# The S5 layer spread over the four retention heads, in quarters of four state tiles, with its tables built on VectorE a step ahead

## The reference, cut to what matters

```
q, k, v, g, u = split(xn @ w_in)                # 512 columns each
o_ret, s_new = retention(rope(q), rope(k), v)   # 4 heads, decay gamma_h, chunkwise
y_ret = silu(g) * head_layernorm(o_ret)
bu = einsum(u, B_bar)                           # S5: 32 groups of 16 channels, 64 complex states
h[t] = a_bar * h[t-1] + bu[t]                   # diagonal, complex
y = gelu(Re(C h) + D u); y_s5 = y * sigmoid(y @ w_glu + b)
x = x + concat(y_ret, y_s5) @ w_out
```

## Time and profile before

| | us |
|---|---|
| median of 3 runs (lowest, highest) | 2462.33 (2460.72, 2467.35) |
| profiled execution: its own time | 2461.94 |
| profiled execution: span | 2460.2 |
| PE busy | 2294.2 |
| DVE busy | 1215.8 |
| POOL busy | 1220.9 |
| ACT busy | 339.8 |

### The profile page before, as it was taken

How to read it: one execution, slowest core, us unless ns; L and a number is a source line. 1 busy time by engine, 2 the same in 40 slices (tenths; PEclk the granted TensorE clock), 3 DMA queues, 4 the chain that set the end, 5 groups by cost and what they waited for, 6 DMA issues and landing times.

```text
span 2460.2 us, 39360 instructions
## 1 busy us (share of the span) xinstructions
PE 2294.2 (93%) x16133; PEld 2123.2 (86%) x16133; DVE 1215.8 (49%) x2104; ACT 339.8 (14%) x578; POOL 1220.9 (50%) x1185
## 2 busy tenths in 40 slices
PE   7968768999999999999999989999989999999997
PEld 7967667997999999999999965687569799999996
DVE  6675576432535263674756425441543327253363
ACT  4211301212200000120110131110212210000001
POOL 5535676642665566666656500022025256655562
PEclk8988889999999999999999977889889999999998
DMA  5212323310222222233333321332131012222221
GB/s 189 85 69 86 103 99 121 138 69 35 70 86 86 86 76 78 85 118 141 130 144 148 113 104 52 131 131 86 56 137 69 35 69 73 83 86 86 84 71 54
DMA packets 36594, 231.27 MB, mean 94 GB/s; under 512 B 4332, under 2 KB 7404, under 8 KB 10864
## 3 DMA queue, kind: packets, MB, share of 16 engines
q1 hardware_dynamic: 21600, 154.15, 17.8%
q10 hardware_dynamic: 14864, 75.21, 7.8%
HBM read 195.50 MB, written 33.85 MB: 93 GB/s over the span
## 4 chain that ended last, share of the span: by engine, by line
PE 79%; DVE 16%; issue 2%; ACT 2%; DMA 0%; ACTq 0%; DVEq 0%
PE psum L513 60%; PE psum L543 14%; PE psum L529 2%; DVE hl L1899 1%; DVE xnl L1425 1%; DVE hh L1895 1%; DVE xc L1964 1%; PE psum L539 1%; DVE tm L1625 1%; DVE ss L1410 0%; DVE hr L1888 0%; DVE hs L1891 0%; DVE bbq L1649 0%; DVE tm L2178 0%; DVE tm L2177 0%
## 5 line engine op out<-in xcount | busy, mean ns | idle before, releaser
L463 POOL TENSOR_SCALAR whi<-raw 128x512 fp32r<-128x512 f32 x584 | 422.7, 724 | 1150.1 <-PE psum L513 1107.2
L465 POOL TENSOR_TENSOR wlo<-raw,whi 128x512 fp32r<-128x512 f32 x584 | 803.0, 1375 | 48.7
L513 PE MATMUL psum<-xnh,whi 128*128 128x288 f32 (+1 forms) x2816 | 625.5, 300 | 64.2 <-DVE xnl L1425 17.8
L513 PE MATMUL psum<-xnl,whi 128*128 128x288 f32 (+1 forms) x2816 | 618.7, 298 | 0.0
L513 PE MATMUL psum<-xnh,wlo 128*128 128x288 f32 (+1 forms) x2816 | 618.2, 298 | 0.0
L513 PEld LDWEIGHTS psum<-xnh,whi 128*128 128x128 f32 x2816 | 465.5, 192 | 74.2 <-issue 52.2
L513 PEld LDWEIGHTS psum<-xnl,whi 128*128 128x128 f32 x2816 | 464.9, 192 | 0.0
L513 PEld LDWEIGHTS psum<-xnh,wlo 128*128 128x128 f32 x2816 | 464.4, 191 | 0.0
L513 PE MATMUL psum<-hh,whi 128*128 128x288 f32 x1024 | 220.2, 296 | 1.6 <-DVE hl L1899 1.6
L513 PE MATMUL psum<-hl,whi 128*128 128x288 f32 x1024 | 219.3, 295 | 0.0
L513 PE MATMUL psum<-hh,wlo 128*128 128x288 f32 x1024 | 219.3, 295 | 0.0
(11 more groups left out here) (395 smaller groups left out, 2735.0 us busy)
## 6 DMA issues: line engine op xcount, KB each, us to landing
raw<-in_w SPq DMA_DIRECT2D x146, 1024.0 KB, 4.7
C<-in_C ACTq DMA_DIRECT2D x4, 1024.0 KB, 4.8
o_cp<-mvt ACTq DMA_DIRECT2D x4, 1024.0 KB, 3.9
o_cs<-C ACTq DMA_DIRECT2D x4, 1024.0 KB, 3.9
t_xc<-xc ACTq DMA_DIRECT2D x3, 1152.0 KB, 6.5
t_z<-mv ACTq DMA_DIRECT2D x3, 1152.0 KB, 4.1
t_q<-mq ACTq DMA_DIRECT2D x3, 1152.0 KB, 4.1
t_k<-mk ACTq DMA_DIRECT2D x3, 1152.0 KB, 4.2
```

Source lines behind the costliest of these rows:

```text
L463: pool.tensor_scalar(whi[:, s, c], raw[:, s, c], 1.0, 1.0, ALU.mult, ALU.mult).then_inc(S("slab_hi"), 1)
L465: ins = pool.tensor_tensor(wlo[:, s, c], raw[:, s, c], whi[:, s, c].bitcast(F32), ALU.subtract)
L513: ins = pe.matmul(bank(g, 2 * m + b)[:, 0:t1 - t0], W[wi][:, kk, m0 + m, :], r[:, kk, t0:t1], start=(at_first and wi == 0 and r is rh), st ...
```

## The change

Each quarter of S5, four of its sixteen state tiles, is put inside one retention head. A head is now, on PE: `score`, transposes of the quarter's input rows, `aux`, memory slab 4h, the quarter's kernel and states (`s5_states`), `out`, slab 4h+1, `mean`, slab 4h+2, `var`, the quarter's output (`s5_out`), slab 4h+3. In head 2 the states come ahead of the slab. DVE does `rotate_back` ahead of `out`'s evacuation, the scan behind it, `rotate_forward` behind the subtraction of the mean, and then the input rows, decay columns and output rows of the next quarter. The states stay in `za` and `zc` (two buffers each), so that `he` and `hf` go. Tables are a quarter in size, the memory tokens have tiles of their own (`memx`), and the decay table of the heads has two buffers that are reloaded. Of the seven doublings four stand behind the evacuation of v's first group, two behind that of its second, and the last behind that of g's first group.

```
@@ schedule() @@
     for h in range(RET_H):
         g("ret", h, "score")
-        if h:
-            g("ret", h - 1, "var")
+        g("s5", h, "T")
         g("ret", h, "aux")
-        for x, m in zip(("out", "mean"), MEM_RET[h]):
-            s("mem", *m)
-            g("mem", *m)
-            g("ret", h, x)
-    memory(8)
-    g("ret", RET_H - 1, "var")
-    memory(9)
-    g("s5T", 0)
-    g("s5T", 1)
-    g("s5K")
...
+        if h != 2:
+            memory(4 * h)
+        g("s5", h, "G")
+        if h == 2:
+            memory(4 * h)
+        g("ret", h, "out")
+        memory(4 * h + 1)
+        g("ret", h, "mean")
+        memory(4 * h + 2)
+        g("ret", h, "var")
+        g("s5", h, "Y")
+        memory(4 * h + 3)
@@ TensorE @@
+            def s5_states(j):
+                g = GR["s5", j, "G"]
+                pe.wait_ge(S("ca_ready"), j + 1)
                 group_open(pe, g)
...
+                pe.wait_ge(S("bt_ready"), j + 1)
...
+            for h in range(RET_H):
+                ret_score(h)
+                s5_transposed(h)
+                ret_aux(h)
+                if h != 2:
+                    memory(MEM_SLABS[4 * h])
+                s5_states(h)
+                if h == 2:
+                    memory(MEM_SLABS[4 * h])
+                ret_out(h)
+                memory(MEM_SLABS[4 * h + 1])
+                ret_mean(h)
+                memory(MEM_SLABS[4 * h + 2])
+                ret_var(h)
+                s5_out(h)
+                memory(MEM_SLABS[4 * h + 3])
@@ ScalarE @@
+            silu(0)
             group_ready(act, GR["rs", "g", 1])
-            act.wait_ge(S("memx_loaded"), 32)
             high_memory(0)
+            silu(1)
             for h in range(RET_H):
-                for m in MEM_RET[h]:
-                    memory_out(m)
+                input_rows_turned(h)
+                memory_out(MEM_SLABS[4 * h])
...
                 act.wait_ge(S("ret_c"), h + 1)
...
+                memory_out(MEM_SLABS[4 * h + 2])
+                rstd(GR["ret", h, "var"], rs)
+                gelu(h)
+                memory_out(MEM_SLABS[4 * h + 3])
+                if h == 1:
+                    act.wait_ge(S("memx1_loaded"), 32)
                     high_memory(1)
@@ VectorE @@
+                for n in ((1, 2, 4, 8), (16, 32))[i]:
+                    doubling(n)
+                    if n in (4, 32):
+                        unit_circle()
...
+            def scan_states(j):
+                A_, C_ = za[:, j % 2, :, 1:W5 + 1], zc[:, j % 2, :, 1:W5 + 1]
+                step(lambda: tt(A_, A_, zb[:], ADD), lambda: tt(C_, C_, zd[:], SUB))
...
+                step(*[lambda z=z: v.tensor_tensor_scan(flat(z[:, j % 2]), flat(rt[:]), flat(z[:, j % 2]), 0.0, MUL, ADD)
+                       for z in (za, zc)])
...
             for h in range(RET_H):
...
+                if h == 0:
+                    output_rows(0)
+                if h == 2:
+                    low_memory(1)
+                    rotate_back(h)
                     ret_y(h - 1)
-                memory_keys(MEM_RET[h][0])
+                    memory_keys(MEM_SLABS[4 * h])
+                else:
+                    if h:
+                        ret_y(h - 1)
+                    memory_keys(MEM_SLABS[4 * h])
+                    rotate_back(h)
...
+                scan_states(h)
+                memory_keys(MEM_SLABS[4 * h + 1])
...
+                rotate_forward(h)
+                memory_keys(MEM_SLABS[4 * h + 2])
+                if h + 1 < RET_H:
+                    input_rows(h + 1)
+                    decay_columns(h + 1)
+                    output_rows(h + 1)
+                else:
+                    split_glu(0)
+                    split_glu(1)
+                memory_keys(MEM_SLABS[4 * h + 3])
```

More of the change, by code:

```diff
@@ L593, in _, with ret_score @@
             pe.wait_ge(S("rope_done"), 2)
[L594 to L598, removed]
+            def ret_score(h):
                 g = GR["ret", h, "score"]
@@ L625, in _, with ret_mean, ret_var @@
                 group_close(ins, g)
-                memory(MEM_RET[h][1])
+            def ret_mean(h):
                 pe.wait_ge(S("ret_o"), h + 1)
[L628 to L632, removed]
+                token_sum(GR["ret", h, "mean"], 2, q[h])
+            def ret_var(h):
+                pe.wait_ge(S("ret_sq"), h + 1)
+                token_sum(GR["ret", h, "var"], 2, sq[:])
@@ L679, in s5_y @@
[L679 to L683, removed]
-                                ins = mm(bank(g, 2 * a + o // 2)[32 * i:32 * i + 32, W5 * (o % 2):W5 * (o % 2) + W5],
-                                         CA[:, c2, 4 * (2 * half + a) + i, o + 1, :], h_[:, 4 * a + i, 0:W5], False,
-                                         o % 2 == 1 and c2 == 1)
@@ L705, in _ @@
-            memory(MEM_SLABS[15])
-            s5_y(1)
+                for b in range(2):
+                    for lag in range(2 * b + 2):
+                        o0 = max(lag, 2 * b)
+                        w = (2 * b + 2 - o0) * W5
+                        for i in range(4):
+                            r = slice(32 * i, 32 * i + 32)
+                            mm(bank(g, b)[r, (o0 - 2 * b) * W5:2 * W5], K32[r, lag, :],
+                               u[r, j].rearrange("p q n -> p (q n)")[:, (o0 - lag) * W5:(o0 - lag) * W5 + w], lag == 0, False)
@@ L1588, in _, with products @@
                 ch.mark(ins, free[g % 2], S("g_scaled"))
+            def products(at, a, b, part, j, n):
+                row = lambda r: sp[:, r:r + n, 4 * j:4 * j + 4].rearrange("p k s -> p s k").unsqueeze(3).to_broadcast([P, 4, n, 16])
+                wide = lambda z: z[:, 4 * j:4 * j + 4, :].unsqueeze(2).to_broadcast([P, 4, n, 16])
+                view = lambda o: tmf[:, o:o + 64 * n].rearrange("p (s k c) -> p s k c", s=4, k=n)
+                t0, t1 = view(at), view(at + 64 * n)
+                step(lambda: tt(t0, wide(a), row(part[0]), MUL), lambda: tt(t1, wide(b), row(part[1]), MUL))
+                return t0, t1
@@ new lines, in output_rows @@
+            def output_rows(j):
+                if j == 0:
+                    v.wait_ge(S("ca_zero"), 1)
+                else:
+                    group_ready(v, GR["s5", j - 1, "Y"])
+                ch.sync()
+                for c2, op in ((0, ADD), (1, SUB)):
+                    t0, t1 = products(0, Cc[:, c2], Cc[:, 1 - c2], (PR, PI), j, Q5 + 1)
+                    for r in range(2):
+                        rows = slice(64 * r, 64 * r + 64)
+                        ch.mark(tt(CA[rows, c2, :, :, 16 * r:16 * r + 16], t0[rows], t1[rows], op))
+                    ch.sync()
+                v.sem_inc(S("ca_ready"), 1)
@@ new lines, in input_rows @@
+            def input_rows(j):
+                if j == 0:
+                    v.wait_ge(S("bb_zero"), 1)
+                ch.sync()
+                for c2, op in ((0, SUB), (1, ADD)):
+                    t0, t1 = products(512 * c2, Bc[:, c2], Bc[:, 1 - c2], (30, 34), j, Q5)
+                    for r in range(2):
+                        rows = slice(64 * r, 64 * r + 64)
+                        dst = bbq[rows, :, c2, :, 16 * r:16 * r + 16].rearrange("p k s c -> p s k c")
+                        ch.mark(tt(dst, t0[rows], t1[rows], op))
+                ch.sync()
+                v.sem_inc(S("bb_ready"), 1)
@@ L1640, in input_rows @@
[L1640 to L1653 removed]
+                ch.mark(tt(xnl[:, h, :], tm[:, 1, :], xnh[:, h, :].bitcast(F32), SUB), S("ret_y"))
```

437 lines of the change are left out of this document (164 added, 273 removed).

## The result

The changed kernel took 2441.99 us (median of 4 runs, 2437.96 to 2445.67) against 2464.84 us of the kernel before beside it: a ratio of 0.9901, 95% interval 0.9886 to 0.9915, so 24 us faster (21 to 28); the two medians differ by 22.9 us. The prediction was 2436.5 us, a ratio of 0.9895 to the 2462.33 us that it started from.

What follows compares the result with a forecast made beforehand. PE was taken to bound the kernel, its waits and half rate being what could go. First memory slab at 176 plus 214.6 puts glu at 390.6, 25.6 earlier: span 2434.6, with 1.7 beyond it and 0.4 for the median 2436.5 us, range 2416 to 2455.

Steps and rivals of the forecast that it cites:

- The front: Up to the first memory slab: the 14.3 us wait goes, DVE's queue takes over, slab at 176, gain 7 us.
- two waits of 3 to 5 us: Sign of being right: PE waits this long ahead of the transposes and of `aux` in head 0.
- Slab 4h+1 to 4h+2: In every head PE has 6.9 us of work, waits 6.9 for POOL's split, and loses 1.8 in half rate.
- T: End of POOL's split of slab 4h+2, drawn out from 8.65 to 13.8 us by DVE's additions, scans and forward rotation.
- the 0.77 us that POOL loses per us of DVE's: Rate at which DVE's own SBUF work delays POOL's split, taken from two windows of the earlier profile.
- The output rows: DVE's work ahead of `Wm`, put at 4.0 us; with the input rows it makes `aux` wait 1.1 in three heads.
- Rival D: DVE bounds a head, PE waits for the forward rotation ahead of `s5_out`: slower, 2462 to 2480 us; chance 0.05.
- The sum: First memory slab to glu: 162 us of PE work plus 52.6 of waits and half rate, 214.6; glu at 390.6.
- A: The forecast itself: splits beside scans take some 13 us, a head some 53; 2427 to 2446 us; chance 0.56.
- B: The split suffers little from DVE, ending between 8.65 and 11 us; 2405 to 2425 us; chance 0.17.
- C: Full exclusion: POOL loses all of DVE's own time, split ends at 17.0 us; 2447 to 2465 us; chance 0.17.
- E: Only the front gains, because of an unseen wait in the heads; 2449 to 2456 us; chance 0.05.

Runs made afterwards that it cites:

- e6: The changed kernel itself, unaltered, measured and profiled once more; ratio 0.9891 to the kernel before.
- e3: The changed kernel without the two additions and two scans of each quarter (S5 output not the reference's); ratio 0.9850 to the kernel before.
- v9: The changed kernel with next head's scores earlier, keys between output-row halves, last doubling behind quarter 0's output rows, final states behind keys; ratio 0.9866 to the kernel before.
- e1: The changed kernel with all seven doublings back between the evacuations of v's two groups; ratio 0.9906 to the kernel before.
- e7: The changed kernel with scaled keys, copies of out and prompt state, and final-state copies given from DVE to ScalarE; ratio 0.9891 to the kernel before.

## Why the prediction was right, step by step

**The front.** Forecast 7 us, first memory slab at 176; measured 4.4, 178.8 (4.3 in e6). That the wait of 14.3 us goes, and that DVE's chain takes its place, was right. A size was off: the doublings of 16 and 32 columns and the small table took 17.7 us (138.0 to 155.8) and not some 13.5. Their second half ran beside the split of the first memory slab, which I had put beside the last doubling. The timeline of DVE shows that it is the small operations that suffer; those from 148.26 to 155.33 took 1.7 us before, with no split beside them, and 7.1 here:

```profile
148.26 1.24 DVE L1512 TENSOR_TENSOR sp<-sp 128x16 f32<-128x16 f32 x2
...
150.13 1.27 DVE L1514 COPY sp<-sp 128x16 f32<-128x16 f32 x1
...
158.73 1.22 DVE L1538 TENSOR_TENSOR tm<-x,sp 128x1024 f32<-128x1024 f32 x1
```

A pair of 16 columns took as long as one operation of 1024 alone. The last doubling and its copies then met no split and took 8.7, not the forecast 11. In place of "two waits of 3 to 5 us" stand one of 10.5 and one of 3.8. The forecast's own times said as much for the first: scores over at 161.1, g's second evacuation at 168.8, so a wait of nearly 8 us.

**Slab 4h+1 to 4h+2.** Forecast T = 13.8 with a wait of 6.9 us; measured 11.4 and 4.4. The mechanism, a split drawn out by DVE's SBUF work, is shown by e3 (8.5 us without it). The step that failed is the 0.77 us that POOL loses per us of DVE's, and with it the forward rotation inside the split. Of the 5.1 us that the forecast added to 8.65, 3.1 were for additions and scans and 2.0 for the rotation. By busy time POOL lost 10.37 less 7.65, 2.7 us, for some 4.4 of DVE's own (two additions at 0.75, two short copies at 0.16, two scans at 1.3 by the earlier trace rows), a rate of 0.6, and nothing for the rotation. DVE in turn loses more than I took (7.7 us for 4.4, a factor 1.75 instead of 1.5), which is what kept the rotation out: it began at 10.6 us and not at 9.8, when POOL's last instruction was under way.

The Trainium skill ("SBUF — State Buffer", section "Who interferes with whom") says that DVE and POOL share one pair of SBUF ports. A DVE instruction with two SBUF inputs and a POOL instruction that reads SBUF contend for it; the one that starts first has it for the whole instruction, and the other is fully blocked. Read as 1.0 us lost for each of DVE's own, this gives T of 13.05 us as an estimate (8.65 and 4.4); the runs show 11.4. The trace agrees that the two take turns. Additions end 0.6 us and scans 1.2 us behind the end of a POOL instruction: POOL's instruction from 254.16 ends at 255.29, DVE's addition from 254.74 at 255.90; POOL's from 257.72 ends at 259.91, DVE's scan from 258.78 at 261.14. It does not agree with the full length as the price. POOL loses what the operation takes alone less 0.3 to 0.4 us: 0.45 on average for an addition of 0.75, 0.97 for a scan of 1.3. In the kernel before, POOL's instructions beside a scan and beside a product of 1160 columns show 2.3 lost for 2.58 and 1.0 lost for 1.37:

```profile
349.49 2.88 POOL L463 TENSOR_SCALAR whi<-raw 128x512 fp32r<-128x512 f32 x1
...
357.64 2.25 POOL L465 TENSOR_TENSOR wlo<-raw,whi 128x512 fp32r<-128x512 f32 x1
```

So 0.77 was the rate of long operations and is too high for quarters. This rule is an estimate from these rows; no run varied the length alone.

For rows and copies the rate is lower still: POOL loses 1.0 us beside output rows (8.67 less 7.65) whose time grows from 3.8 to 8.2 us on DVE, and 0.5 beside four copies. The 3.8 are the same eight operations where no split runs, in v9 (timeline of DVE, half of them):

```profile
283.69 0.89 DVE L1577 TENSOR_TENSOR tm<-Cc,sp 128x320 f32<-128x320 f32 x2
284.62 1.00 DVE L1590 TENSOR_TENSOR CA<-tm 64x320 f32<-64x320 f32 x2
```

**Costs that I did not charge.** The output rows were put at 4.0 us ahead of `Wm`, as if alone; beside the split they take 8.2. In head 0 this is a wait of 3.1 us ahead of the states instead of 1.7, in heads 1 and 3 the transposes wait 1.5 us for keys that stand behind the rows, and `s5_out` waits 2.0 and 1.0 us in heads 0 and 2 for keys behind the rotation. Rival D had named that last place, for another reason.

**The sum.** From the first memory slab to glu 214.65 us, forecast 214.6. This agreement is partly luck: PE's waits there are 37 us (all waits from 130 to 425 us are 53.3, less 10.5 and 3.8 in the front and 1.7 behind glu; forecast 41.6, and 1.5 for signals), PE's busy time is 177.3 (forecast 162 and 9.5 of half rate). The four waits for the split were 17.6 us and not 27.6, the one ahead of glu 4.8 and not 6.5, all others 15 and not 7.5. The 6 us more of busy time are at least in part half rate that I left out, such as 4.33 us instead of 2.65 for the lag part of `s5_out` in head 0. So errors of 12 us one way and of 13 the other cancelled, with the 1.5 for signals. Glu begins at 393.4 instead of 390.6, all of it by the front.

**The rivals.** A's figures for a head did not come: T is 11.4, the wait 4.4 and not 5 to 8, and the split 10.7 us from its first instruction to its last and not 12 to 14. That is nearer to B (T between 8.65 and 11, "splits under 11 us") than to A, though the total came out as A's. C (17 us) and D did not come, and E is refuted by e1: the heads alone gave 18.4 us. A's range was also added up wrongly: 6 us less to 10 more is 2430.5 to 2446.5, not 2427 to 2446.

## What to carry to other kernels

Two engines that work in SBUF at once are priced by the operation, not by one rate: take scans and other long two-operand work away from a split, and leave PSUM work there. SBUF copies and small operations cost POOL little, but DVE much, so they belong there only where DVE has time. A shorter queue is worth something only where its engine is late; elsewhere it moves its work into a neighbour's critical stretch, as in e7. When a unit is cut into quarters, look at its single buffers: in heads 0 and 2 DVE waits for PE to release `CA`, 2.07 and 0.52 us.

## What I had not expected of the hardware

Beside a split, a DVE copy of 4 columns takes 1.15 us where the next one takes 0.16, and a pair of 16 columns 1.24 instead of 0.26 (in e1, where no split runs): an operation is held up once, whatever its own size, until the POOL instruction in flight ends (0.62 to 1.29 us alone). The rows above show it: the copy of 4 columns begins at 255.93 and ends at 257.08, POOL's instruction from 255.37 ends at 257.05. That is the reason why many small operations beside POOL are dear for DVE and cheap for POOL, and why a chain of them has to be priced by their number and not by their time. It is read from ends that fall together; no run here isolates it.
